# Index keys and head weights in one projection tile, the 64-token output product on both column halves, first modulation chunks copied by ScalarE

## The chip, the cores and the metric

One NeuronCore of one Trainium2 chip runs the whole program; the other cores are idle. The metric is the device time of one execution in microseconds (us), the median over several runs.

## What is computed

The reference is one layer of a hybrid streaming encoder on 512 prompt tokens and 64 sample tokens (the latter with 256 cached positions), model width 1024. In short:

```python
mod = silu(c) @ w_ada + b_ada                      # six vectors of 1024 per stream
h = rmsnorm(x) * (1 + sc1) + sh1
qa, ka, va, qi, ki, wi, qb, kb, vb, qc, kc, vc = split(h @ w_in)
# A: indexer. score[t, s] = sum_h wi[t, h] / sqrt(8) * relu(qi[t, h] . ki[s] / 8), top-k keys, softmax
# B: stick-breaking attention   C: differential attention
x = x + g1 * (concat(oa, ob, oc) @ w_out)
h2 = rmsnorm(x) * (1 + sc2) + sh2
x = x + g2 * (shared expert + top-8 of 64 experts)(h2)
y = rmsnorm(x) * g_final
```

The index keys ki have 64 columns of w_in, the head weights wi 8, and in w_in the 8 stand right behind the 64. The rows of ki, ka, va, kb, vb, kc and vc are outputs too.

## The kernel before

**Layout.** Tokens stand in the free dimension, features in the partitions: h_hi and h_lo (the float32 activations split in two parts) are 128 x 8 x 576. The input projection goes by *tiles* of 128 columns of w_in, named in TILES: first ("ki", 0), then ("wi", 0), four of "qi", and the rest, 30 in all. The tile of ki holds its 64 columns twice, so that both halves of the partitions hold the keys; the tile of wi takes 128 columns of w_in of which only the first 8 are used. Each tile is 48 matmuls of 288 columns (three products of high and low parts, 8 blocks of k, two banks), lines 1457 to 1459.

**Around a tile.** SyncE (SP) loads the weights of 512 KB into a ring of four stages (line 838), ScalarE (ACT) rounds them to w_hi (line 1172), GpSimd (POOL) forms w_lo (line 722; for tile 0 it is VectorE, DVE), TensorE (PE) multiplies, ACT moves both banks to SBUF (line 1214). For a tile whose rows are wanted, PE turns it back to rows with five transposes (lines 1540 and 1544), which wait for both banks to be in SBUF, and ACT takes these out of PSUM (lines 1238 and 1241). make_schedule() writes one order of steps; every engine walks through it and does its own part. The first score step waits for the projection tiles of index queries, and DVE for the rows of wi.

**The first chunks of the modulation.** Before the projection, four chunks n = 0 to 3 give shift and scale of the first norm. For each, PE multiplies silu(c) with 2 MB of w_ada (line 1485; four groups of 32 columns of the array side by side), DVE copies the 128 x 512 result out of PSUM into the single buffer mod_rows (line 2019, shown as run), PE turns it into partitions with matmuls of two columns (line 1496), and DVE adds the bias (line 2032). Then ACT writes h_hi for two blocks (line 1178, four instructions), and DVE computes the same in float32 (hf, line 2038) and the low part h_lo (line 2043). DVE has all of it in one queue: copy(n), modulation(n), the two blocks of n, then copy(n+1). After chunk 1, DVE also forms w_lo of tile 0. The w_ada buffers are three: chunk 3 is loaded into that of chunk 0, after PE has read it (line 821). Of PE, modulation(n), turn(n), modulation(n+1) stand in this order, and projection 0 behind turn(3).

**The output projection.** out_product(t) multiplies o_t with w_out for token tile t (four of 128 tokens, the last, t = 4, of 64), for two halves c of the 1024 columns, into banks (2t + c) mod 4, c outside and k inside (line 1744). DVE multiplies each half by g1 (line 2257, part) and adds it to x (line 2260); ACT then forms the inverse root (line 1350 and on), and DVE the normalized rows h2_rows, which PE turns (line 1755). POOL clears x_got after the last product (wo_full 10, lines 1091 to 1095). Behind this stand the router (line 1769), the choice of experts on DVE (lines 2282 and on), the lists of units, and 72 MoE steps of four units of 32 tokens (lines 1919, 1937, 1955).

Of the kernel before, what the change touches and what calls it, by code (L numbers as in the profile page):

```python
# [14 lines left out]
P = 128  # L15
# [7 lines left out]
HD = 64  # L23
# [106 lines left out]
TILES = ([("ki", 0), ("wi", 0)] + [("qi", i) for i in range(4)]  # L130
# [6 lines left out]
ROWS = ("ki", "wi", "ka", "va", "kb", "vb", "kc", "vc")  # L137
# [12 lines left out]
def make_schedule():  # L150
# [19 lines left out]
    project(TILES[:6])  # L170
    s.append(("cache", "i", 0))
    tiles = list(TILES[6:21])
# [46 lines left out]
    softmax_units([("a", h, t) for t in (1, 2, 3, 4, 0) for h in range(H_A)], TILES[21:27])  # L219
# [4 lines left out]
    project(TILES[27:])  # L224
# [69 lines left out]
def build(nc, io):  # L294

    ctx = ExitStack()
    with ctx:
# [394 lines left out]
        row_sources = [st[1] for st in rows_steps if TILES[st[1]][0][0] in "vw"]  # L692
# [224 lines left out]
        def _(pool):  # L917
# [33 lines left out]
            def store_rows(step):  # L951
                name, j = TILES[step[1]]
                if name == "wi":
                    return
# [32 lines left out]
            def pad(key):  # L987

                g, h, t = key
                if key in (("a", 0, 1), ("c", 0, 0)):  # L990
                    if g == "c":
                        pool.wait_ge(av_done, len(stick_no))
                    pool.wait_ge(proj_taken, 2 * (12 if g == "a" else N_IN))
# [146 lines left out]
        def _(act):  # L1140
# [50 lines left out]
            root()  # L1191
            for q in range(N_FIRST):
                tr.wait_taken(act, ("ada", q))
                modulated(2 * q)
                modulated(2 * q + 1)
                if q == 1:
                    split_high(0)
            split_high(1)

            def evacuate_projection(n):  # L1200
                name, j = TILES[n]
                for b in range(2):
                    act.wait_ge(proj_full, 2 * n + b + 1)
                    if name in ("wi", "va", "vb", "vc"):
# [5 lines left out]
                    else:  # L1210
                        dst = feat(SLOT[name] + j)
                        if b == 0 and name in ("qc", "kc"):
                            qk.wait_full(act, last_score)
                    nc.scalar.activation(dst[:, HALF * b:HALF * b + HALF], bank[b][:, 0:HALF], ACT.Copy,
                                         scale=SCALE_A if name == "qb" else 1.0).then_inc(proj_taken, 1)

            def evacuate_rows(step):
# [3 lines left out]
                if name == "wi":  # L1221
                    w, scale = N_IDX, N_IDX ** -0.5
                    dst = [wi_rows[:, 0:4, :], wi_rows[0:N_SAMPLE, 4, :]]
                elif name[0] == "k":
# [5 lines left out]
                else:  # L1230
# [5 lines left out]
                    dst = [v[:, 0:4, P * j:P * j + P], v[0:N_SAMPLE, 6, P * j:P * j + P]]  # L1236
                tr.wait_full(act, key[0])
# [214 lines left out]
        def _(pe):  # L1452
# [114 lines left out]
            for step in SCHEDULE:  # L1567
# [17 lines left out]
                elif kind == "score":  # L1585
                    t, h = key
                    if t == 1 and h == 0:
                        pe.wait_ge(proj_taken, 2 * 6)
# [7 lines left out]
                elif kind == "qk":  # L1596
                    g, h, t = key
                    if (g, h, t) == ("a", 0, 1):
                        wait_cached("a")
                        pe.wait_ge(proj_taken, 2 * 12)  # L1600
# [136 lines left out]
            def out_product(t):  # L1737
                c0, n = tokens(t)
                for c in range(2):
# [264 lines left out]
        def _(dve):  # L2004
# [10 lines left out]
            def copy_modulation(n):  # L2015
                dve.wait_ge(ada_rows, n + 1 if n < 4 else 4 * (n - 3) + 4)
                if n:
# [541 lines left out]
```

## Time and profile before

| What | Value |
|---|---|
| median of 3 runs | 1239.8 us (1235.46 to 1242.24) |
| the profiled execution | 1229.7 us, its span 1227.7 us |
| PE busy | 1106.3 us, 90% of the span |
| DVE busy | 520.7 us, 42% |
| ACT busy | 371.9 us, 30% |
| POOL busy | 367.3 us, 30% |
| mean granted TensorE clock | 0.975 |

The busy shares are averages over stages; the rows further down give single stretches. Times of rows count from the first instruction of the span. A matmul on float32 operands appears as two instructions in the trace, so that a count of x16 there is eight matmuls of the program.

### The profile page before, as it was taken

To read this page: it belongs to the slowest core of one execution; us is meant where nothing else is said; L and a number is where in the kernel's file an instruction comes from. 1 tells how busy PE (TensorE), PEld (TensorE's weight loads), DVE (VectorE), ACT (ScalarE), POOL (GpSimd) and SP (SyncE) were. 2 spreads that over 40 slices of the span, in tenths; PEclk is the share of its full clock that TensorE was granted. 3 is DMA by queue.
4 is the path that set the end of the run, shared out by engine and by line. 5 is a ranking of instruction groups with operands and counts; after the bars stand their busy time and mean duration, and the time that the engine had idled before them with its cause. 6 is when DMAs were issued, how large, how long until landed. Compare 5 with 4: busy or idle time off the path is not lost.

```text
span 1227.7 us, 24855 instructions
## 1 busy us (share of the span) xinstructions
PE 1106.3 (90%) x9769; PEld 673.1 (55%) x9769; DVE 520.7 (42%) x1293; ACT 371.9 (30%) x908; POOL 367.3 (30%) x464
## 2 busy tenths in 40 slices
PE   3899998899889988899899889999999999999696
PEld 1698896676574555545445444545555555555242
DVE  5517892133426567624552624323233332222155
ACT  3433432233335457601103212222222222222211
POOL 2233333423321043130112423434343434343100
PEclk9899999999999999999989998999999999999898
DMA  9322225633444000030054796969797969676596
GB/s 363 121 86 78 82 80 207 222 109 123 156 172 140 1 1 2 1 112 35 28 221 152 249 376 204 371 251 378 260 377 253 383 241 385 231 297 228 185 422 215
DMA packets 58563, 239.37 MB, mean 195 GB/s; under 512 B 22686, under 2 KB 22766, under 8 KB 46414
## 3 DMA queue, kind: packets, MB, share of 16 engines
q1 hardware_dynamic: 27936, 181.73, 40.2%
q0 software_dynamic: 30512, 56.06, 13.2%
q8 instruction: 78, 1.28, 0.4%
q14 instruction: 37, 0.30, 0.1%
HBM read 292.57 MB, written 47.40 MB: 277 GB/s over the span
## 4 chain that ended last, share of the span: by engine, by line
PE 68%; DMA 16%; DVE 7%; issue 4%; ACT 3%; POOL 2%; SPq 0%; POOLq 0%; DVEq 0%; ACTq 0%
PE bank L1937 14%; PE bank L1955 9%; DMA x_got<-x_dram,idx_tok 8%; PE bank L1744 6%; PE bank L1457 5%; PE bank L1459 5%; PE bank L1458 5%; DMA pairs<-pair_dram 4%; PE bank L1919 4%; PE bank L1563 3%; PE bank L1639 2%; PE bank L1485 1%; PE bank L1683 1%; PE bank L1838 1%; DMA pair_dram<-out_rows,idx_pair 1%
## 5 line engine op out<-in xcount | busy, mean ns | idle before, releaser
L1937 PE MATMUL bank<-slot,xt 128*32 128x256 f32 x4608 | 262.2, 379 | 14.9 <-issue 10.1
L1937 PEld LDWEIGHTS bank<-slot,xt 128*32 128x32 f32 x4608 | 152.5, 110 | 141.8 <-issue 54.3
L1457 PE MATMUL bank<-h_hi,w_hi 128*128 128x288 f32 x480 | 145.3, 303 | 0.0
L1458 PE MATMUL bank<-h_lo,w_hi 128*128 128x288 f32 x480 | 141.7, 295 | 0.0
L1459 PE MATMUL bank<-h_hi,w_lo 128*128 128x288 f32 x480 | 141.6, 295 | 0.0
L1955 PE MATMUL bank<-slot,hid_t 128*32 128x512 f32 x1152 | 139.2, 601 | 0.8 <-ACT hid_t L1424 0.8
L1119 POOL DMA_INDIRECT pair_dram<-out_rows,idx_pair x72 | 73.1, 1016 | 169.0 <-DVE out_rows L2429 156.1
L722 POOL TENSOR_TENSOR w_lo<-w_stage,w_hi 128x1024 fp32r<-128x1024 f32 x29 | 69.6, 2400 | 127.3 <-ACT w_hi L1172 127.3
L2429 DVE COPY out_rows<-bank 128x512 f32<-128x512 f32 x72 | 49.8, 691 | 115.3 <-PE bank L1955 75.0
L1418 ACT ACTIVATE sg<-bank 128x128 f32<-128x128 f32 x72 | 20.0, 277 | 252.0 <-PE bank L1937 251.8
L1457 PEld LDWEIGHTS bank<-h_hi,w_hi 128*128 128x128 f32 x480 | 90.5, 189 | 6.8 <-issue 6.3
L2423 DVE TENSOR_TENSOR hid<-sg,bank 128x128 f32<-128x128 f32 x72 | 20.6, 287 | 169.2 <-ACT sg L1418 160.7
L1458 PEld LDWEIGHTS bank<-h_lo,w_hi 128*128 128x128 f32 x480 | 90.6, 189 | 0.8 <-issue 0.5
L1102 POOL DMA_INDIRECT x_got<-x_dram,idx_tok x72 | 73.3, 1019 | 56.9 <-DVE idx_tok L2400 33.5
L1459 PEld LDWEIGHTS bank<-h_hi,w_lo 128*128 128x128 f32 x480 | 90.4, 188 | 0.0
L1111 POOL DMA_INDIRECT slot<-in_w_moe,idx_w x48 | 49.5, 1032 | 130.0 <-DVE out_rows L2429 76.5
L1919 PE MATMUL bank<-ident,x_got 128*128 128x128 f32 x576 | 76.3, 276 | 11.9 <-DMA x_got<-x_dram,idx_tok 11.8
L1744 PE MATMUL bank<-w_out_sb,o_t 128*128 128x512 f32 (+1 forms) x160 | 71.6, 608 | 2.5 <-DVE o_t L2189 2.5
L1919 PEld LDWEIGHTS bank<-ident,x_got 128*128 128x128 f32 x576 | 65.3, 142 | 15.2 <-DMA x_got<-x_dram,idx_tok 13.9
L1430 ACT COPY out_rows<-bank 128x512 f32<-128x512 f32 x72 | 42.2, 586 | 102.2 <-PE bank L1955 54.4
L2417 DVE COPY xt<-bank 128x512 f32<-128x512 f32 x72 | 49.8, 691 | 53.2 <-PE bank L1919 53.1
L1283 ACT ACTIVATE p_work<-p_work,n_max 128x256 f32<-128x256 f32 (+4 forms) x80 | 44.5, 557 | 62.8 <-DVE n_max L2158 62.6
(366 smaller groups left out, 1537.1 us busy)
## 6 DMA issues: line engine op xcount, KB each, us to landing
slot<-in_w_moe SPq DMA_DIRECT2D x65, 1536.0 KB, 8.7
w_stage<-in_w_ada SPq DMA_DIRECT2D x32, 512.0 KB, 4.4
pairs<-pair_dram SPq DMA_DIRECT2D x16, 1024.0 KB, 9.9
w_stage<-in_w_in SPq DMA_DIRECT2D x30, 512.0 KB, 3.3
resid<-in_w_ada SPq DMA_DIRECT2D x2, 2048.0 KB, 12.9
w_out_sb<-in_w_out SPq DMA_DIRECT2D x1, 4096.0 KB, 14.8
g_bc<-mod_dram SPq DMA_DIRECT2D x6, 512.0 KB, 8.9
o_t<-in_x_t SPq DMA_DIRECT2D x4, 576.0 KB, 5.7
```

The source lines that it names most:

```text
L722: e.tensor_tensor(w_lo[:, n % 2], staged(("w", n)), w_hi[:, n % 2].bitcast(F32), ALU.subtract)\
L1102: g.indirect_dma_start(x_got[:, i % 4, :], None, x_dram, bass.IndirectOffsetOnAxis(ap=idx_tok[:, i:i + 1], axis=0), bounds_check=NT - 1, o ...
L1119: g.indirect_dma_start(pair_dram, bass.IndirectOffsetOnAxis(ap=idx_pair[:, i:i + 1], axis=0), out_rows[:, i % 2, :], None, bounds_check=NT ...
L1457: mm(out, hi_w, hi_x, start=first, stop=False)
L1458: mm(out, hi_w, lo_x, start=False, stop=False)
L1459: return mm(out, lo_w, hi_x, start=False, stop=last)
L1744: ins = mm(bank[i % 4][0:n, :], o_t[:, k, c0:c0 + n], w_out_sb[:, k, 512 * c:512 * c + 512], start=(k == 0), stop=(k == KD - 1))
L1919: ins = nc.tensor.transpose(bank[k // 4][:, P * (k % 4):P * (k % 4) + P], x_got[:, i % 4, P * k:P * k + P], ident[:, :])
L1937: ins = mm(bank[2 + i % 2][r, 0:2 * P], xt[:, i % 2, k, r], slot_of(place_no)[:, 2 * P * k:2 * P * (k + 1)], start=(k == 0), stop=(k == KD ...
L1955: ins = mm(bank[4 + 2 * (i % 2) + c][r, :], hid_t[:, i % 2, r], slot_of(place_no)[:, 2 * D + 512 * c:2 * D + 512 * c + 512], start=True, s ...
L2417: v.tensor_copy(xt[:, i % 2, 4:8, :], bank[1][:, :].rearrange("p (k c) -> p k c", k=4)).then_inc(xt_dve, 1)
L2429: v.tensor_copy(out_rows[:, i % 2, 512:D], bank[5 + 2 * (i % 2)][:, :]).then_inc(out_dve, 1)
```

## The change

Three things change. First, TILES has no ("wi", 0): the tile of ki takes 128 plain columns of w_in from the first of ki on, so that its result holds ki in partitions 0 to 63 and wi in 64 to 71. ACT writes ki from each bank twice (to partitions 0 to 63 and 64 to 127 of its feature slot), and the whole bank into v_t; the turning takes 72 rows of v_t, and ACT takes head weights and keys out of the turned banks separately. Second, the copies of chunks 0 to 3 of the modulation out of PSUM go from DVE to ACT. Third, out_product(4) puts the two halves of the columns into partitions 0 to 63 and 64 to 127 (of two banks), with k outside and c inside. The constants that count tiles follow.

```diff
-TILES = ([("ki", 0), ("wi", 0)] + [("qi", i) for i in range(4)]
+TILES = ([("ki", 0)] + [("qi", i) for i in range(4)]
...
@@ scalar engine, before the projection
+            def copy_modulation(n):
+                act.wait_ge(ada_rows, n + 1)
+                if n:
+                    act.wait_ge(ada_full, n)
+                nc.scalar.copy(mod_rows, tr_bank[tr.bank(("ada", n))][:, :]).then_inc(rows_copied, 1)
+
+            copy_modulation(0)
             for q in range(N_FIRST):
                 tr.wait_taken(act, ("ada", q))
                 modulated(2 * q)
                 modulated(2 * q + 1)
+                if q + 1 < N_FIRST:
+                    copy_modulation(q + 1)
                 if q == 1:
                     split_high(0)
             split_high(1)
@@ evacuate_projection(n)
-                    if name in ("wi", "va", "vb", "vc"):
+                    if name in ("ki", "va", "vb", "vc"):
...
+                    if name == "ki":
+                        for r in (0, HD):
+                            nc.scalar.copy(feat(SLOT["ki"])[r:r + HD, HALF * b:HALF * b + HALF], bank[b][0:HD, 0:HALF])
                     nc.scalar.activation(dst[:, HALF * b:HALF * b + HALF], bank[b][:, 0:HALF], ACT.Copy,
@@ evacuate_rows(step)
+                if name == "ki":
+                    w = HD + N_IDX
+                    tr.wait_full(act, key[0])
+                    both = src[0][:, 0:4 * w].rearrange("p (t c) -> p t c", t=4)
+                    nc.scalar.activation(wi_rows[:, 0:4, :], both[:, :, HD:w], ACT.Copy, scale=N_IDX ** -0.5)
+                    nc.scalar.copy(dst[0], both[:, :, 0:HD]).then_inc(tr_free[tr.bank(key[0])], 1)
...
@@ tensor engine, turn_rows(step)
-                src = feat(SLOT[name] + j) if name[0] == "k" else v_t[:, row_sources.index(n) % 2, :]
-                r = {"wi": N_IDX, "ki": HD}.get(name, P)
+                src = v_t[:, row_sources.index(n) % 2, :] if n in row_sources else feat(SLOT[name] + j)
+                r = HD + N_IDX if name == "ki" else P
@@ out_product(t)
+                if t == 4:
+                    for c in range(2):
+                        pe.wait_ge(part_ready, 5 + c)
+                    for k in range(KD):
+                        for c in range(2):
+                            ins = mm(bank[c][n * c:n * c + n, :], o_t[:, k, c0:c0 + n], w_out_sb[:, k, 512 * c:512 * c + 512],
+                                     start=(k == 0), stop=(k == KD - 1))
+                            if k == KD - 1:
+                                ins.then_inc(wo_full, 1)
+                    return
@@ vector engine
             for q in range(N_FIRST):
-                copy_modulation(q)
                 modulation(q)
...
+                    r = slice(n * c, n * c + n) if t == 4 else slice(0, n)
+                    v.tensor_tensor(part[0:n, c, :], bank[i % 4][r, :], g1_bc[r, stream(t), cols], ALU.mult)\
```

## Rows read from the trace of the kernel before

**Rows 1.** The page: chain of work that ended last, shares by engine.

```profile
PE 68%; DMA 16%; DVE 7%; issue 4%; ACT 3%; POOL 2%; SPq 0%; POOLq 0%; DVEq 0%; ACTq 0%
```

**Rows 2.** Windows: length, busy PE, PEld, DVE, ACT, POOL (xcount), clock, DMA share, GB/s.

```profile
150.00:187.00 37.00, 36.00 (x272) 34.13 (x271) 33.90 (x79) 13.62 (x27) 13.29 (x9) 1.00 0.28 87
523.50:600.80 77.30, 77.30 (x217) 35.51 (x217) 27.63 (x43) 8.26 (x21) 10.15 (x52) 0.97 0.19 65
659.20:1160.00 500.80, 470.21 (x6416) 252.69 (x6416) 162.66 (x389) 120.80 (x288) 188.93 (x185) 0.99 0.78 287
```

**Rows 3.** Chain that ended last, 15 to 61 us: start, length, what.

```profile
23.25 0.70 DVE run L2019
24.00 1.88 PE bank L1496 x8
...
50.81 0.82 ACT resid L1214 x2
```

**Rows 4.** Timeline of PE before the projection: start, length, instruction, [idle before].

```profile
16.80 3.64 PE L1485 MATMUL bank<-resid,silu_c 128*32 128x512 f32 x16 [0.82 <-DMA resid<-in_w_ada]
...
31.42 1.92 PE L1485 MATMUL bank<-ada_third,silu_c 128*32 128x512 f32 x16
...
43.63 1.05 PE L1496 MATMUL bank<-of_stream,run 128*128 128x2 f32 x8 [1.00 <-DVE run L2019]
44.54 0.38 PE L1457 MATMUL bank<-h_hi,w_hi 128*128 128x288 f32 x1
```

**Rows 5.** Window of PE alone: length, busy (xcount), granted clock, DMA share, GB/s.

```profile
40.00:42.00 2.00, 2.00 (x16) 0.50 0.01 4
```

**Rows 6.** Timelines of ACT and DVE, 23 to 40 us.

```profile
26.17 2.18 ACT L1178 ACTIVATE h_hi<-o_t,mod 128x512 fp32r<-128x512 f32 x4 [8.49 <-DVE mod L2032]
...
33.88 1.03 ACT L1172 CAST w_hi<-w_stage 128x1024 fp32r<-128x1024 f32 x1
...
29.02 0.76 DVE L2043 TENSOR_TENSOR h_lo<-hf,h_hi 128x576 fp32r<-128x576 f32 x1
...
35.32 1.22 DVE L722 TENSOR_TENSOR w_lo<-w_stage,w_hi 128x1024 fp32r<-128x1024 f32 x1
```

**Rows 7.** SP timeline, and the same loads' KB and us to landing.

```profile
5.12 0.45 SPq L821 DMA_DIRECT2D ada_third<-in_w_ada  x1
20.48 0.33 SPq L821 DMA_DIRECT2D resid<-in_w_ada  x1
...
ada_third<-in_w_ada SPq DMA_DIRECT2D x1, 2048.0 KB, 23.0
...
resid<-in_w_ada SPq DMA_DIRECT2D x1, 2048.0 KB, 12.6
```

**Rows 8.** Timeline of PE: first matmuls of projection 1 (wi) and of 2.

```profile
52.12 0.40 PE L1457 MATMUL bank<-h_hi,w_hi 128*128 128x288 f32 x1
...
59.62 0.40 PE L1457 MATMUL bank<-h_hi,w_hi 128*128 128x288 f32 x1
```

**Rows 9.** Timeline of ACT: a copy of 128 x 512 out of PSUM.

```profile
630.28 0.59 ACT L1390 COPY unit_value<-bank 128x512 f32<-128x512 f32 x1 [11.01 <-PE bank L1810]
```

**Rows 10.** Groups by form, 586.8 to 601 us: xcount, busy us, mean ns, idle before.

```profile
L1744 PE MATMUL bank<-w_out_sb,o_t 128*64 128x512 f32 x32 | 13.9, 594 | 0.0
L1744 PEld LDWEIGHTS bank<-w_out_sb,o_t 128*64 128x64 f32 x32 | 4.3, 137 | 8.9 <-issue 8.9
```

**Rows 11.** Timeline of PE: one MoE step's down products, four column groups of 32.

```profile
675.96 1.92 PE L1955 MATMUL bank<-slot,hid_t 128*32 128x512 f32 x16
```

**Rows 12.** Timelines of DVE and POOL behind the output projection.

```profile
600.86 0.68 DVE L2257 TENSOR_TENSOR part<-bank,g_bc 64x512 f32<-64x512 f32 x1 [5.46 <-PE bank L1744]
...
604.63 2.51 DVE L2282 TENSOR_SCALAR score<-score 128x64 f32<-128x64 f32 x1 [0.27 <-ACT score L1368]
...
603.58 3.52 POOL L1095 MEMSET x_got<- 128x4096 f32 x1
```

**Rows 13.** The page's groups: turning of the gathered tokens in the MoE stage.

```profile
L1919 PE MATMUL bank<-ident,x_got 128*128 128x128 f32 x576 | 76.3, 276 | 11.9 <-DMA x_got<-x_dram,idx_tok 11.8
```

More of the change, by code:

```diff
@@ L168, in project_with_ada @@
             s.append(("rows", tile[k]))
-    project(TILES[:6])
+    project(TILES[:5])
     s.append(("cache", "i", 0))
-    tiles = list(TILES[6:21])
+    tiles = list(TILES[5:20])
     for t in (1, 2, 3, 4):
@@ L217, in softmax_units @@
             project([k])
-    softmax_units([("a", h, t) for t in (1, 2, 3, 4, 0) for h in range(H_A)], TILES[21:27])
+    softmax_units([("a", h, t) for t in (1, 2, 3, 4, 0) for h in range(H_A)], TILES[20:26])
     s += [("cache", "c", 0), ("cache", "c", 1)]
@@ L223, in make_schedule @@
     s += [("pad",) + units[0], ("pad",) + units[1]]
-    project(TILES[27:])
+    project(TILES[26:])
     for i in range(len(units) + 4):
@@ L690, in softplus @@
             return sp_buf[:, :, :].rearrange("p s c -> p (s c)")[:, c:c + w]
-        row_sources = [st[1] for st in rows_steps if TILES[st[1]][0][0] in "vw"]
+        row_sources = [st[1] for st in rows_steps if TILES[st[1]][0] in ("ki", "va", "vb", "vc")]
         def pad_rows(key, m):
@@ L1236, in evacuate_rows @@
                     dst = [v[:, 0:4, P * j:P * j + P], v[0:N_SAMPLE, 6, P * j:P * j + P]]
+                if name == "ki":
[4 more added lines that the diff above has]
+                    nc.scalar.copy(dst[0], both[:, :, 0:HD]).then_inc(tr_free[tr.bank(key[0])], 1)
+                    tr.wait_full(act, key[1])
+                    nc.scalar.activation(wi_rows[0:N_SAMPLE, 4, :], src[1][0:N_SAMPLE, HD:w], ACT.Copy, scale=N_IDX ** -0.5)
+                    nc.scalar.copy(dst[1], src[1][0:N_SAMPLE, 0:HD]).then_inc(tr_free[tr.bank(key[1])], 1)
+                    return
                 tr.wait_full(act, key[0])
@@ L2108, in _ @@
                         for half in range(2):
-                            tr.wait_taken(dve, ("rows", 1, half))
+                            tr.wait_taken(dve, ("rows", 0, half))
                     qk.wait_taken(dve, step)
@@ L2256, in add_out @@
                     dve.wait_ge(wo_full, i + 1)
-                    v.tensor_tensor(part[0:n, c, :], bank[i % 4][0:n, :], g1_bc[0:n, stream(t), cols], ALU.mult)\
+                    r = slice(n * c, n * c + n) if t == 4 else slice(0, n)
+                    v.tensor_tensor(part[0:n, c, :], bank[i % 4][r, :], g1_bc[r, stream(t), cols], ALU.mult)\
                         .then_inc(part_ready, 1)
@@ L2541 @@
         c = COL[name] + P * j
-        tiles.append(np.concatenate([w_in[:, :, c:c + HD]] * 2, axis=2) if name == "ki" else w_in[:, :, c:c + P])
+        tiles.append(w_in[:, :, c:c + P])
     laid_out["w_in"] = np.stack(tiles).transpose(0, 2, 1, 3).reshape(N_IN, P, D)
```

21 lines of the change are left out of this document (8 added, 13 removed).

## The prediction

> **What bounds the kernel now.** I read the chain that ended last first: 68% of it is TensorE [rows 1]. Then the windows. Between 150 and 187 us, in the stage of scores and top-k, PE is busy 36.0 of 37 us and DVE 33.9; in the output projection PE is busy for all of 77.3 us; in the MoE stage for 470 of 501 us [rows 2]. So what is taken off PE in these stages counts nearly in full. The start is another matter: there the chain goes by turns over DVE's copy out of PSUM (23.25, 0.70 us), PE's turning (24.00, 1.88 us) and DVE's arithmetic [rows 3], and PE stands still between its products [rows 4]. What is saved there counts if projection 0, which starts at 44.54 us [rows 4], starts earlier, since PE is dense from then on. The three parts of the change lie in three places, one behind another, so their effects add.
>
> **Part 1, the first chunks.** Before, copy(n+1) stands on DVE behind all its work for chunk n, and PE cannot turn before it. After, ACT makes the copy; behind it on ACT stand the h_hi of the next chunk, and, behind copy(2), the rounding of tile 0's weights, for which DVE waits. I go through it with the durations of before; ACT's copy of 128 x 512 from PSUM takes 0.59 us [rows 9].
> PE's product of chunk 0 ends at 16.80 + 3.64 = 20.44 [rows 4]; ACT is free, its copy ends at 21.1; PE's turning (1.88) at 23.0. DVE is done with the normalization at 23.25, where its copy began [rows 3], so its bias follows at 23.25, not at 25.9: 2.6 us gained. PE's product of chunk 1 runs from 23.0 to 26.6, the copy to 27.2, the turning (1.05 to 1.88 us by the clock [rows 3, 4]) to 28.3. Chunk 2's weights land at 5.12 + 23.0 = 28.1 [rows 7], in time; its product, 1.92 us at the full clock [rows 4], ends at 30.3. ACT's four h_hi of chunk 1 take 2.18 us [rows 6] and end at 30.8, copy(2) at 31.4, the rounding (1.03) at 32.5. DVE's chunk lasts from 25.88, where the turning ended, to 29.78, that is 3.9 us [rows 3, 6], here from 28.3 to 32.2; then w_lo, 1.22 us [rows 6], to 33.7. PE turns chunk 2 until 32.5. Chunk 3 goes into chunk 0's buffer, whose load is issued at 20.48 in either kernel, since PE's first product does not move, and lands 12.6 us later, at 33.1 [rows 7]; product to 35.0. DVE starts chunk 2 at 33.7, its bias is done at 33.9, h_hi at 36.1, copy(3) at 36.7, turning at 37.8. Projection 0 starts there and not at 44.54: **6.7 us**. The last h_lo, 3.9 us later at 41.7, comes before projection 0 wants the last block of k, 7/8 of its some 6.3 us in, at 43.3.
> The bound on the other side is the clock. From 40 to 42 us the granted clock was 0.50, the 1.2 GHz level, after PE had stood since 33.3 [rows 5, 4]; a product takes 3.64 and a turning 1.88 us at that level. With the low level for chunk 3 alone it ends at 33.1 + 3.64 + 0.6 + 1.9 = 39.3, 5.3 us gained; with the low level from turning 1 on (29.1, 32.8, 33.4, 35.3, 38.9, 39.5, 41.4) 3.1 us. Because the new pauses of PE, 1.0 to 1.3 us, are shorter than those of before, I take 6.5.
> The Trainium skill (TensorE: Matmul & The Clock Gate, the clock gate part) says that the array starts at 1.2 GHz and gets to 2.4 GHz once it was kept busy; the products of 3.64 and of 1.92 us agree, and by that rule the low ends above would need longer pauses than I find.
>
> **Part 2, keys and head weights.** From the first matmul of tile "wi" to that of the next tile are 59.62 - 52.12 = 7.50 us [rows 8]: its 48 matmuls and its turning, both on PE's path. All of it goes, with one rounding on ACT, one w_lo on POOL, one load of 512 KB and two evacuations, which lie beside PE's work: nothing. Added are four ACT copies of 288 columns from PSUM, two for each bank, ahead of the copies into v_t for which the turning waits. PE stands behind them in order, nothing covers this. Two such copies took 0.82 us, the second in part waiting for its bank [rows 3]: 0.41 each, 1.6 in all, is the upper bound; by columns, 0.59 x 288/512 = 0.33 [rows 9], 1.3 in all, the lower. I take 1.4, the middle. The split taking of the turned rows adds nothing on PE's path: the next tile's w_hi begins some 2 us later on ACT, and after 1.03 us there and POOL's w_lo it is wanted only a whole tile later. DVE's wait for the head weights is met sooner, as rows 0 is an earlier step. Part 2: 7.5 - 1.4 = **6.1 us** (5.9 to 6.2).
>
> **Part 3, the output product of 64 tokens.** It takes 13.9 us for 32 instructions, one each 0.434 us, back to back, though it uses 64 of 128 columns [rows 10]. No row shows two groups of 64 columns side by side. The nearest is the MoE down product: 16 instructions of 512 columns in four groups of 32 last 1.92 us [rows 11], 0.12 each against 0.434, so that four run at once. Two groups then give 13.9/2 = 6.95, a gain of 6.9 us; the other end is no overlap at all, gain 0. I take 6.9, since the alternation of groups is that of rows 11. Both halves are now full only at the end, at 593.9, and DVE's first half (two operations of 0.68 us), formerly beside PE's second, comes behind: ACT's inverse root moves by 5.5 us only. But this path is not what ends last: DVE's first operation on the router's scores took 2.51 us, until 607.14, because POOL was clearing x_got until 603.58 + 3.52 = 607.10 [rows 12], and this clearing starts by wo_full 10, so it moves by the full 6.9, to 600.2. The scores, formerly there at 604.6, are there at 599.1, still before it. **6.9 us** reach the choice of experts. The new wait for the banks, for the adds of t = 2, is long met: there is a whole tile of PE work between. That DVE reads partitions 64 to 127 costs nothing: as many columns.
> The Trainium skill (TensorEngine Tiling (Array Packing), Restrictions) speaks against this part: column tiling switches off the fast weight load, and a change of the tiling drains the array. If every one of the 32 loads, 0.137 us each now [rows 10], stood open, 4.4 us would come back and part 3 would give 2.5. In rows 11 the loads of the four groups are hidden.
>
> **Sum.** 6.5 + 6.1 + 6.9 = 19.5 us. In the profiled execution 1229.7 becomes 1210.2; the median of the runs stands 10.1 us above that execution, so I forecast 1239.8 - 19.5 = **1220.3 us**, 1.6% less.
>
> **The rivals.**
> (a) *The halves do not overlap.* Part 3 gives 0: both halves end at 600.8, and ACT's path, 1.4 later, still ends at 606.0, before the clearing. 1239.8 - 12.6 = 1227.2 us. For it: no row with groups of 64. Against: rows 11. 0.08.
> (b) *The weight loads stand open* between the halves: part 3 gives 2.5, 1224.7 us. For it: the loads of 64 columns are twice as wide as those of rows 11. 0.05.
> (c) *The clock stays low in the start*: part 1 gives 3.1, 1223.7 us. 0.10.
> (d) *Hidden anyway*: DVE, 33.9 of 37 us busy in the top-k stage [rows 2], sets its end, and not from the scores' start; then parts 1 and 2 are lost and only 6.9 are left: 1232.9 us. Against: DVE begins with the first scores, which move with the tiles. 0.04.
> (e) *Slower*: the MoE stage. There DMA is busy 78% of the time [rows 2], and PE has waited 11.8 us in all for gathered tokens [rows 13]. The change touches nothing there, but starts it 19.5 us sooner; if the gathers fell otherwise among the weight loads and came later than PE wants them, it would cost. To be slower by 0.5% it must lose 19.5 + 6.2 = 25.7 us, waits three times as long as now, which decides it; at 26 us 1246.3. Against: all issues there hang on PE's and DVE's own progress and move along. 0.03.
>
> **How the numbers follow.** The forecast has 0.70, its own range being 1216 to 1224: part 1 down to 5.3, part 2 5.9 to 6.2, and the spread of the runs shown, 0.3 to 0.4% about their median. The range, 1213 to 1230, takes in (a), (b), (c) and that spread; (d) and (e) are left out. About 0.5% (6.2 us) is what a measurement of this kernel can tell from no change. Faster by more: the forecast, (a), (b), (c), 0.93. Within: (d), 0.04. Slower: (e), 0.03.
>
> **What would show it.** Projection 0 starts near 38 us (41 by (c)); the gap between its last matmul and the first turning is 0.5 + 1.4 us; 29 tiles; the 32 instructions of out_product(4) end in some 7 us (9 to 12 by (b), 13.9 by (a)), and the clearing of x_got ends that much sooner after its start. The distance from the choice of experts to the end stays. A MoE stage of another length, or a projection 0 that starts after 42, would make the prediction wrong.

## The result, and the profile of the changed kernel

The changed kernel takes **1234.1 us** (median of 22 runs, 1218.5 to 1243.1), the kernel before, run beside it, 1240.3 (22 runs, 1232.7 to 1250.8). The ratio is 0.9921 [0.9894, 0.9948]: faster, where 1.6% less was forecast, and outside the range of 1213 to 1230. This ratio leaves out as slow the eight of the 22 changed executions that lie more than 1.5% above the fastest of them, 1218.5, and none of the kernel before, so it flatters the change: the two medians are 6.2 us apart, a ratio of 0.995, and a second series of the changed kernel (again, below) gives 0.9956. So the direction was right, and of the 19.5 us that were forecast some 6 to 7 came. The profiled execution took 1227.08 us, its span 1225.4, against 1229.7 and 1227.7 before.

**First the three places.** The page of the changed kernel, the shares of its chain, and the waits for gathered tokens (before: [rows 1, 13]):

```profile
PE 72%; DMA 16%; DVE 4%; issue 3%; ACT 3%; POOL 2%; SPq 0%; DVEq 0%; POOLq 0%; ACTq 0%
...
L1949 PE MATMUL bank<-ident,x_got 128*128 128x128 f32 x576 | 78.3, 281 | 19.6 <-DMA x_got<-x_dram,idx_tok 19.6
```

PE's timeline, the changed kernel (start us, us, operation, idle before in brackets):

```profile
28.81 3.64 PE L1504 MATMUL bank<-ada_third,silu_c 128*32 128x512 f32 x16 [0.99 <-DMA ada_third<-in_w_ada]
...
34.94 3.64 PE L1504 MATMUL bank<-resid,silu_c 128*32 128x512 f32 x16
...
39.28 1.86 PE L1515 MATMUL bank<-of_stream,run 128*128 128x2 f32 x8 [0.71 <-ACT run L1195]
41.01 0.59 PE L1476 MATMUL bank<-h_hi,w_hi 128*128 128x288 f32 x1
...
51.00 0.47 PE L1559 MATMUL bank<-ident,v_t 72*128 72x72 f32 x4 [2.01 <-ACT v_t L1225]
...
584.15 7.09 PE L1764 MATMUL bank<-w_out_sb,o_t 128*64 128x512 f32 x32
...
596.74 3.45 PE L1799 MATMUL bank<-r_w,h_t 128*128 128x64 f32 x16 [2.69 <-ACT h_t L1377]
```

The timelines of ACT, POOL and DVE, the changed kernel:

```profile
48.63 0.79 ACT L1224 COPY resid<-bank 64x288 f32<-64x288 f32 x2 [4.06 <-PE bank L1478]
49.75 0.78 ACT L1224 COPY resid<-bank 64x288 f32<-64x288 f32 x2
...
593.99 3.52 POOL L1094 MEMSET x_got<- 128x4096 f32 x1
...
596.83 0.72 DVE L2311 TENSOR_SCALAR score<-score 128x64 f32<-128x64 f32 x1 [1.64 <-ACT score L1387]
```

The same turning in the kernel before:

```profile
51.68 0.46 PE L1540 MATMUL bank<-ident,resid 64*128 64x64 f32 x4 [0.50 <-ACT resid L1214]
```

Part 1: projection 0 starts at 41.01 us instead of 44.54 [rows 4], near the 41.4 of case (c), because the later products and the last turning run at 3.64 and 1.86 us, the low level. Part 2: the four copies take 0.79 + 0.78 us, and the gap before the first turning is 2.01 us, 1.5 more than the 0.50 of before. Part 3: 7.09 us for 13.9 [rows 10]. DVE's first operation on the scores takes 0.72 us where it took 2.51 [rows 12].
**Then the stages.** The windows of PE between the same events, before and after (window and its length, busy time, granted clock, DMA share, GB/s): from projection 0 to the first scores, the middle (before only), from the output product to the choice of experts, the lists, the MoE stage, and the sums (before only).

```profile
44.50:86.20 41.70, 40.06 (x304) 1.00 0.24 80
86.20:354.20 268.00, 248.20 (x1669) 0.98 0.37 125
...
523.50:624.30 100.80, 95.28 (x321) 0.96 0.21 68
624.30:659.20 34.90, 34.06 (x127) 0.90 0.61 227
659.20:1165.70 506.50, 470.24 (x6417) 0.99 0.78 286
1165.70:1227.70 62.00, 50.59 (x112) 0.91 0.85 320
```

```profile
41.00:77.90 36.90, 34.26 (x250) 0.96 0.24 75
...
520.60:615.20 94.60, 90.27 (x321) 0.94 0.21 73
615.20:650.20 35.00, 34.12 (x131) 0.90 0.63 228
650.20:1162.50 512.30, 474.23 (x6416) 0.97 0.77 283
```

The scores come 8.3 us earlier (77.9 for 86.2), the choice of experts 9.1, the MoE stage begins 9.0 us earlier, and then it lasts 5.8 us longer (512.3 for 506.5), with the clock at 0.97 for 0.99. "A MoE stage of another length" is among the prediction's own signs of being wrong. In this pair of traces it is the largest single loss, but the profile of the control run below, with nothing changed, has a MoE stage of 510.5 us. One pair of traces does not settle it.

### The profile page after: what moved, and what is told of

It reads as the page before. It is cut to its first block, busy times and chain, and to the rows that moved or that the text cites. A ratio compares the mean times of both kernels' runs of the same rounds, so it can differ in the third digit from the quotient of the medians.

```text
span 1225.4 us, 24745 instructions
## 1 busy us (share of the span) xinstructions
PE 1105.5 (90%) x9716; PEld 672.6 (55%) x9716; DVE 517.3 (42%) x1289; ACT 372.8 (30%) x913; POOL 364.6 (30%) x463
## 4 chain that ended last, share of the span: by engine, by line
PE 72%; DMA 16%; DVE 4%; issue 3%; ACT 3%; POOL 2%; SPq 0%; DVEq 0%; POOLq 0%; ACTq 0%
PE bank L1967 15%; PE bank L1985 9%; DMA x_got<-x_dram,idx_tok 8%; PE bank L1774 5%; PE bank L1949 5%; PE bank L1476 4%; PE bank L1478 4%; PE bank L1477 4%; PE bank L1582 3%; DMA pairs<-pair_dram 2%; PE bank L1658 2%; PE bank L1504 2%; DMA ada_third<-in_w_ada 2%; PE bank L2027 2%; PE bank L1868 2%
## 5 line engine op out<-in xcount | busy, mean ns | idle before, releaser
L1985 PE MATMUL bank<-slot,hid_t 128*32 128x512 f32 x1152 | 142.6, 614 | 0.7 <-ACT hid_t L1443 0.7
L1476 PE MATMUL bank<-h_hi,w_hi 128*128 128x288 f32 x464 | 141.7, 305 | 0.0
L1477 PE MATMUL bank<-h_lo,w_hi 128*128 128x288 f32 x464 | 138.3, 298 | 0.0
L1478 PE MATMUL bank<-h_hi,w_lo 128*128 128x288 f32 x464 | 138.2, 298 | 0.0
L1949 PE MATMUL bank<-ident,x_got 128*128 128x128 f32 x576 | 78.3, 281 | 19.6 <-DMA x_got<-x_dram,idx_tok 19.6
L1985 PEld LDWEIGHTS bank<-slot,hid_t 128*32 128x32 f32 x1152 | 30.7, 111 | 59.2 <-issue 58.1
```

What stands on the lines that cost most here:

```text
L1476: mm(out, hi_w, hi_x, start=first, stop=False)
L1477: mm(out, hi_w, lo_x, start=False, stop=False)
L1478: return mm(out, lo_w, hi_x, start=False, stop=last)
L1949: ins = nc.tensor.transpose(bank[k // 4][:, P * (k % 4):P * (k % 4) + P], x_got[:, i % 4, P * k:P * k + P], ident[:, :])
L1985: ins = mm(bank[4 + 2 * (i % 2) + c][r, :], hid_t[:, i % 2, r], slot_of(place_no)[:, 2 * D + 512 * c:2 * D + 512 * c + 512], start=True, s ...
```

## The experiments

Two figures recur. For every execution the record has the time and the mean granted clock. The **low time** of an execution is 2 x (1 - mean clock) x its time, the us spent at 1.2 GHz. Over the 133 executions of the kernel before (control's and those beside each experiment) the time rises by 0.35 us for each us of low time (correlation 0.81), over 34 of the changed kernel by 0.40 (0.92). I take off 0.40 us for each and call the rest **work**. Such a slope alone does not show that the clock costs the time: a longer wait can add to both. The fillings further down, which take low time away and leave the kernel's own work as it is, are the test of that.

The low time has a gap at the start. In every profile the record of the clock begins at a rise to 2.4 GHz, 16 to 30 us into the span, and the time ahead of it counts as full clock. In before's profile that is at 29.5 us, and there a product takes 3.64 us, the value of the low level, in a window that is given at 1.00:

```profile
24.00:29.00 5.00, 5.00 (x24) 1.00 1.01 429
...
25.80 3.64 PE L1485 MATMUL bank<-feat,silu_c 128*32 128x512 f32 x16
```

Over the ten profiles with DVE's copies the record begins at 23.5 us on average, over the ten with ACT's at 19.2, so some 4 us of a difference in low time between such kernels can be this alone.

The table has means over all executions, with their standard errors. The series ran on five chips, each with the kernel before beside it; its means there lie between 1239.6 and 1242.8 us, and its low time between 87.5 and 97.6. A difference of 1 to 3 us to the pooled mean is therefore less certain than the errors in the table say.

```
kernel              executions   us              low time       work
before and control  133          1240.6 +- 0.5    89.3 +- 1.1   1204.9
changed              34          1233.8 +- 0.9   105.9 +- 2.2   1191.4
only_copies          12          1231.5 +- 1.1    79.0 +- 2.7   1199.8
only_tile            12          1245.2 +- 1.6   106.9 +- 4.4   1202.5
tile_stored          12          1244.8 +- 1.4   110.2 +- 3.1   1200.8
only_halves          12          1237.4 +- 1.8    98.9 +- 4.7   1197.9
tile_held            12          1245.8 +- 1.8    97.8 +- 3.3   1206.7
tile_loaded          12          1241.4 +- 1.3    97.5 +- 3.5   1202.4
before_late          12          1247.7 +- 1.0    90.9 +- 3.0   1211.3
before_plus          12          1240.8 +- 1.9    91.9 +- 3.8   1204.1
halves_filled        12          1234.2 +- 1.2    92.0 +- 2.8   1197.4
warm_start            6          1225.7 +- 2.8    84.6 +- 4.5   1191.9
warm_moe              6          1227.4 +- 2.0    91.7 +- 4.2   1190.7
both_warm             6          1227.9 +- 1.6    87.6 +- 3.7   1192.9
copies_halves         6          1230.5 +- 2.7    92.0 +- 6.2   1193.7
copies_halves_2       6          1233.8 +- 3.5    97.2 +- 7.8   1194.9
copies_halves_warm    6          1230.3 +- 2.2    77.1 +- 4.4   1199.5
all_filled            6          1222.8 +- 2.0    71.8 +- 2.9   1194.1
```

**The parts alone, and the kernel before once more.** Each keeps one part of the diff; for the copies, for example:

```diff
+            def copy_modulation(n):
+                act.wait_ge(ada_rows, n + 1)
+                if n:
+                    act.wait_ge(ada_full, n)
+                nc.scalar.copy(mod_rows, tr_bank[tr.bank(("ada", n))][:, :]).then_inc(rows_copied, 1)
...
             for q in range(N_FIRST):
-                copy_modulation(q)
                 modulation(q)
```

> The kernel before with the first part alone (the first chunks' copies on ACT). Theory A: projection 0 starts 3 to 6.7 us sooner than 44.5, but up to 3 us of it are lost in its own first matmuls at the low clock: the time 0 to 6 us less, ratio 0.995 to 1.000. Rival B: clock low from 24 to 44 us, projection 0 starts at 41, net gain 1 us or none, ratio 0.999 to 1.003.

> The kernel before with the second part alone (keys and head weights in one tile). Theory A: the stretch from projection 0 to the first score product 36 to 36.5 us where it was 41.6 in the profile, with part 2's 6.0 us in it, and the time 6 us less, ratio 0.995. Rival C (a gain ahead of the MoE stage is eaten there by waits for gathered tokens): the same at the scores, but the MoE stage longer and the time less by under 3 us, ratio 0.998 or more.

> The kernel before with the third part alone (the 64-token output product on both halves of the columns). Theory A: 7.1 us for the 32 instructions, the clearing of x_got 6.8 us sooner after the start of the output projection, and the time 6.8 us less, ratio 0.9945. Rival C: the same up to the choice of experts, then a longer MoE stage, ratio 0.998 or more.

> The kernel before, unchanged, as its own control. The 35 executions of it that ran beside the last four kernels had a mean granted clock of 0.965, that is 88 us at the low level (twice 1 - clock, times the time), and 1240.7 us on average; the profile that the prediction went by had 0.975, 61 us and 1229.7. Theory D (that profile was a lucky execution, and MoE waits for gathered tokens of 17 to 23 us are the rule of both kernels): ratio 0.998 to 1.002, and in this profile the MoE stage is 510 to 519 us (506.5 in the first) with waits of 15 us or more. Rival B (the changed kernels bring the waits): the MoE stage again near 506 us with 12 us of waits.

> The changed kernel once more, to see what of its profile is the same in another execution. Theory A (the three gains are real, and the granted clock falls otherwise in each execution): the stretch from the start of projection 0 to the first score product again 36 to 37 us, 41.6 before; the 32 instructions of the 64-token product again 7.1 us, 13.9 before; but the start of projection 0 between 38 and 41.5 us and the low-clock stretches elsewhere than in the first profile, and the time between 1218 and 1240 us. Rival B (the change itself brings the low clock and the longer waits for gathered tokens): the clock is 0.50 again from about 24 to 44 us and from 509 to 526 us, the waits for gathered tokens are again near 20 us (12 before), and the time 1230 to 1240 us.

Ratios to before: copies 0.9941 [0.9911, 0.9971], tile 1.0043 [1.0006, 1.0081], halves 0.9969 [0.9932, 1.0005], control 0.9998 [0.9966, 1.0030], the whole change again 0.9956 [0.9922, 0.9990]. From the means: copies -9.1 us, tile +4.4 (with tile_stored, which differs only in memory), halves -3.2; their sum, -7.9, agrees with the -6.8 of the whole. So the effects do add, about, and the terms of tile and halves are wrong. In work they are -5.1, -3.3 and -7.0, near the forecast 6.5, 6.1 and 6.9 for the first and the last; the rest goes with low time: -10, +19 and +10 us of it. The whole change has 16.5 us more low time than before, at 0.40 us each 6.6 us given back, of 13.5 of work.

The windows of PE of the control, at the start and for the MoE stage:

```profile
24.00:44.00 20.00, 16.31 (x72) 0.50 0.66 269
...
660.10:1170.60 510.50, 471.29 (x6416) 0.98 0.78 284
```

And of only_tile, from projection 0 to the scores, the middle, the MoE stage and the sums:

```profile
44.50:81.60 37.10, 34.45 (x251) 0.95 0.24 75
81.60:350.40 268.80, 247.27 (x1669) 0.98 0.37 125
...
655.90:1174.90 519.00, 477.28 (x6416) 0.97 0.76 279
1174.90:1238.20 63.30, 50.92 (x112) 0.93 0.83 313
```

In the tile alone the stage up to the scores is 4.6 us shorter, as part 2 says, the middle 0.8 longer, the MoE stage 12.5 longer than in before's profile and 8.5 longer than in the control's, the sums 1.3 longer. But the length of the MoE stage says little about the tile: over all twenty profiles it goes from 506 to 521 us, and the ten without the merged tile average 513.4 us, the ten with it 515.3; before_late below, without it, has 520.6.

**Where the tile's loss comes from.** First where w_in lies in memory: the merged tile drops one of 30 tiles, and everything stored behind could move. tile_stored keeps 30 in memory and skips one.

```diff
-                src = io["w_ada"][n // 4][:, D * (n % 4):D * (n % 4) + D] if kind == "ada" else io["w_in"][n]
+                src = io["w_ada"][n // 4][:, D * (n % 4):D * (n % 4) + D] if kind == "ada" else io["w_in"][n + (n > 0)]
...
+        if name == "ki":
+            tiles.append(w_in[:, :, COL["wi"]:COL["wi"] + P])
```

> The kernel with the merged tile alone, but w_in stored with its 30 tiles as before, the second never read, so that all tensors lie in DRAM where they lay. The merged tile alone had 107 us at the low clock on average against 88 before, and a ratio of 1.004 where its own gain was to give 0.995. Theory E (the place of the expert weights in DRAM is what makes transfers and so PE's pauses longer): low clock back to about 88 us, ratio 0.995. Theory A (the earlier start only shifts the stages against the clock's rise and fall, the place is of no matter): low clock again 100 to 110 us, ratio 1.000 to 1.006.

1.0030 [0.9994, 1.0065], mean 1244.8: the same loss. The place in memory is out.

Then whether PE time ahead of the MoE stage counts at all. tile_held is only_tile, and before_late the kernel before, each with one more tile's 48 matmuls on PE, into a bank that nobody reads. They take 6.4 us at 2.4 GHz; the 7.50 us of [rows 8] hold the turning too. The edit of tile_held (before_late has the same ahead of projection 2):

```diff
+                    if step[1] == 1:
+                        pe.wait_ge(w_lo_ready, 2)
+                        for b in range(2):
+                            for k in range(KD):
+                                three(bank[4][:, 0:HALF], w_hi[:, 1, k, :], w_lo[:, 1, k, :],
+                                      h_hi[:, k, halves(b)], h_lo[:, k, halves(b)], k == 0, k == KD - 1)
```

> The kernel with the merged tile alone, but with the removed tile's 48 matmuls made all the same (same operands' shapes, into a bank nobody reads) behind projection 0, so that PE's time to the scores is the old one. The merged tile alone took 1245.0 us on average over 24 executions against 1240.7 of the kernel before, with 109 us at the low clock against 88. Theory G (it is the earlier position of all later stages, that is another phase of the same pauses, which brings the low clock): low clock back to 85 to 92 us, time 1241 to 1243. Theory H (something else in the merged tile, its copies or the pause behind projection 0): low clock stays 100 to 110 us, and the time is the 6.4 us of these matmuls above it, 1250 to 1252.

> The kernel before with 48 more matmuls of a projection tile (dense, into a bank nobody reads) ahead of projection 2, which takes 6.4 us of PE. The kernel before is at 1241.1 us on average. Theory A (PE's time ahead of the MoE stage counts in full): 1246.5 to 1248.5, low clock 86 to 94 us. Theory K (the MoE stage's length depends on the execution and on how the stages meet the clock's changes so strongly that some 6 us ahead of it do not show): 1240 to 1244.

before_late: 1.0058 [1.0030, 1.0086], +7.1 +- 1.1 us, and its low time is that of before. PE time there counts in full, 7.1 for 6.4. tile_held: 1.0023 [0.9987, 1.0059], mean 1245.8. Giving the merged tile these 6.4 us of PE back costs 0.8 +- 2.1 us, with 10.8 us less low time: the saving is there, and low time comes with it. Neither expectation fits whole: the low time came down as theory G says, the time did not. Against the pooled mean tile_held is 5 us above before, with 8 us more low time; against the 17 executions of before on its own chip it is 3.0 +- 2.2 us above, with the same low time (0.3 +- 4.0 us more). So it is not shown that anything else in the merged tile costs.

Then the number of transfers. before_plus adds one load of 512 KB to the kernel before (ACT waits for it much later, ahead of the first kb tile), tile_loaded to only_tile, which thus has as many as before:

```diff
+                if i == 4:
+                    sp.wait_ge(ada_rows, 2)
+                    sp.dma_start(feat2[:, :, :].rearrange("p k n -> p (k n)")[:, 8 * NT - D:8 * NT], io["w_in"][0])\
+                        .then_inc(extra_in, 16)
```

> The kernel before with one more transfer of 512 KB on SP's queue, early, into columns that are free then, and nothing else. Theory L (the number of transfers on that queue ahead of the MoE stage changes how its transfers run): the mean moves by 3 us or more either way, or the low clock by 10 us or more. Otherwise: 1239.5 to 1242.5, low clock 86 to 94 us.

> The merged tile alone, with the transfer it saves still made, at the same place in SP's queue as in before_plus. The merged tile alone: 1245.0 us on average, low clock 109 us. Theory L: back to the 1235 to 1237 us that its 6 us of PE time should give, low clock about 90. Otherwise: 1243 to 1247, low clock 100 to 110.

0.9994 [0.9957, 1.0030] and 1.0025 [0.9992, 1.0059]. On before it does nothing; on only_tile the mean is 3.6 us less than with both forms of the tile, two standard errors, and each against before on its own chip it is 2.4 us less, about one: not enough to name a cause.

One candidate shows in the traces, and no run tests it: the longer pause behind projection 0. With the clock at 1.00 throughout, the stretch from projection 0 to the scores takes 41.6 us without the merged tile and 35.5 with it, 6.1 less. Before is in [rows 4] and in the windows above; tile_stored has

```profile
43.70:79.20 35.50, 32.93 (x249) 1.00 0.24 79
```

But of the seven profiles with the merged tile whose projection 0 runs at full speed (tile_held aside, which has other work there), four have 3.4 us of low clock just behind this pause, and their stretch takes 37.1 us, like only_tile's:

```profile
53.15 0.34 PE L1550 MATMUL bank<-ident,v_t 72*128 72x72 f32 x2 [2.01 <-ACT v_t L1216]
...
53.50:56.50 3.00, 3.00 (x15) 0.50 0.13 37
```

None of the five such profiles without the merged tile has it; there the pause is 0.50 us. That is about 0.9 us on average; what the tile loses beyond it stays open.

**Fillings on the changed kernel.** Matmuls on constants, written to a bank that is overwritten before anybody reads it, keep PE busy where it waits anyway. warm_start has them in the pauses between the first chunks, warm_moe at one wait for gathered tokens:

```diff
+            def busy(out, n):
+                for _ in range(n):
+                    mm(out, neg_ones[:, :], ident[:, :], start=True, stop=True)
+            busy(bank[4][:, 0:P], 4)
             for n in range(N_FIRST):
                 modulation(n)
+                busy(bank[4][:, 0:P], 3)
                 turn_modulation(n)
+                busy(bank[4][:, 0:P], 3 if n < N_FIRST - 1 else 0)
...
             def turn_x(i):
+                if i == 11:
+                    pe.wait_ge(xt_act, i)
+                    pe.wait_ge(xt_dve, i)
+                    for _ in range(28):
+                        mm(bank[0][:, 0:P], ident[:, :], ident[:, :], start=True, stop=True)
```

> The changed kernel with matmuls whose result nobody reads (128 x 128 constants, 4 ahead of the first modulation product, 3 behind each product and each turning but the last), so that PE does not pause there. If it is the low clock that takes back part 1's gain: the clock is 1.00 from chunk 1 on, a modulation product takes 1.9 us, projection 0 starts by 38.5 us with matmuls at full speed, and the time is 4 to 6 us less than that of the changed kernel, ratio to before 0.991. If the clock does not follow this filling: start of projection 0 at 41 to 43, time as the changed kernel or 1 to 2 us more.

> The changed kernel with 28 such matmuls (6 us at the full clock) ahead of the turning of MoE step 11, where PE waits 8 us for gathered tokens and the clock is low for 10 us behind it. If that pause is what brings the low clock: no low stretch behind step 11, on average 10 us less at the low clock than the changed kernel's 106, and 2.5 to 5 us less time. If the low clock there has another cause: low stretch as before, time unchanged within 1 us.

> The changed kernel with both fillings, at the start and ahead of MoE step 11. Alone they had 1225.7 and 1227.4 us on average against 1233.8 of the changed kernel. If both fillings act by the low clock they remove: 1219 to 1222 us on average, low clock near 70 us (85 and 92 alone), ratio to before 0.983.

Ratios to before: 0.9892 [0.9838, 0.9946], 0.9884 [0.9828, 0.9940], 0.9885 [0.9840, 0.9930]. Against the changed kernel that is -8.1 +- 2.9, -6.4 +- 2.2 and -5.9 +- 1.8 us, with 21, 14 and 18 us less low time, and the work is the same as the changed kernel's within 1.5: what the fillings gain goes with the low time that they remove, at about the slope of above. The two together show no more than each alone, where 1219 to 1222 us were expected. In warm_start's own profile 6.8 us of low clock stay (from 26.7 us), and projection 0 starts at 39.2, not by 38.5; in both_warm's it starts at 38.0. In the changed kernel's windows the wait at step 11 of the MoE stage is followed by low clock:

```profile
720.00:725.00 5.00, 1.00 (x17) 0.83 1.02 424
725.00:730.00 5.00, 0.91 (x4) 0.50 0.98 392
730.00:735.00 5.00, 5.00 (x41) 0.65 0.30 103
```

and its timeline has the wait itself, 8.09 us for the gather:

```profile
729.09 1.97 PE L1949 MATMUL bank<-ident,x_got 128*128 128x128 f32 x8 [8.09 <-DMA x_got<-x_dram,idx_tok]
```

The same rows with the filling (warm_moe) show a high clock where the filling runs, and low later, in the rest of the wait:

```profile
725.00:730.00 5.00, 5.00 (x63) 1.00 0.99 413
735.00:740.00 5.00, 3.73 (x20) 0.66 0.45 158
```

The kernel before has this wait too (control: 8.08 us at 739.55). It was not made by the change. All profiles without this filling have 6.8 to 10.2 us of low clock in and behind it, but for before_late, which waits 3.95 us there and has 3.4; the four with the filling have 3.4 or none.

**Parts 1 and 3 without part 2.** If part 2 loses some 4 us, leaving it out should win.

> The first and the third part without the merged tile. If the parts' measured effects add (copies -9.2 us, halves -3.3, tile +4.3 against the mean of the kernel before, 1240.7): 1228 us on average, 5.6 us less than the whole change (1233.8), low clock near 90 us. If each part's raw effect is only the luck of its stages' positions and the work saved is what counts: 1236 to 1240 us, slower than the whole change by the 4.3 to 6 us that the tile saves.

> The first and third part without the merged tile once more, for more executions: 1230.5 us on average over the first six. If leaving the tile out is worth what the single parts said: 1228 to 1231, below the whole change's 1233.8. If not: 1233 to 1238.

> The first and the third part with both fillings and without the merged tile. If the merged tile costs time in itself: 5 us less than with it (both_warm). If the tile only shifted pauses: 4 to 6 us more than both_warm.

The first gave 0.9898 [0.9840, 0.9956], but its second series, for which the record has no ratio, a mean of 1233.8; the 12 together 1232.1, which can't be told from the changed kernel's 1233.8. With the fillings, 0.9886 [0.9837, 0.9934], 2.4 +- 2.8 us more than both_warm with part 2: it has 77.1 us of low time for 87.6, while its work is 6.6 higher, about part 2's forecast. (Without the fillings the work differs by 2.9 only, 1194.3 for 1191.4, so work does not add up exactly either.) So the tile loses when it is alone, and I could not show that it loses beside the other parts.

**Part 3's own pause.** halves_filled is only_halves with

```diff
             turn_h2(3)
+            pe.wait_ge(part_ready, 8)
+            for _ in range(11):
+                mm(bank[3][:, 0:P], ident[:, :], ident[:, :], start=True, stop=True)
             route(3)
```

> The third part alone with 11 matmuls on constants (2.3 us at the full clock, result read by nobody) in the pause of PE behind the turning of h2 tile 3, where it waits 2.7 us for ACT. In both kernels with this part and the low clock profiled as 17.1 us there, the lists' stage took 40.0 us, not 35.0. If this pause brings that low clock: no low stretch at 594 to 600 us, the lists' stage 35.0 us, low clock 88 to 92 us on average (98.9 without the filling), time 1233.5 to 1235 (1237.4 without). If not: 40.0 us again, time 1237 to 1239.

The same place in PE's timeline of the kernel before:

```profile
604.53 2.00 PE L1769 MATMUL bank<-r_w,h_t 128*128 128x64 f32 x16 [0.90 <-ACT h_t L1358]
```

PE's timeline, and windows of PE that begin there and at the lists, of only_halves:

```profile
599.27 3.67 PE L1780 MATMUL bank<-r_w,h_t 128*128 128x64 f32 x16 [2.69 <-ACT h_t L1358]
...
595.00:615.00 20.00, 17.07 (x92) 0.83 0.37 92
600.00:605.00 5.00, 5.00 (x17) 0.50 0.00 0
617.70:657.70 40.00, 39.12 (x131) 0.79 0.55 199
```

And of halves_filled, a window and the timeline:

```profile
595.00:615.00 20.00, 18.33 (x130) 1.00 0.39 118
...
599.44 2.62 PE L1847 MATMUL bank<-ident 128*128 128x128 f32 x22
602.29 2.00 PE L1780 MATMUL bank<-r_w,h_t 128*128 128x64 f32 x16 [0.23 <-ACT h_t L1358]
```

Before, PE waited 0.90 us for h_t. With 7 us less of product in front of this place it waits 2.69, since ACT's evacuation, inverse root and scaling are as long as they were. Behind it the clock is at 0.50 from 600 to 605; with the pause filled it stays at 1.00, and the router's product takes 2.00 us for 3.67. From the output product to the MoE stage it was 135.7 us before, 129.6 in the best profiles with the halves, and 134.2 in only_halves, where the stage of the lists took 40.0 us at a clock of 0.79 (for 34.9 at 0.90); six of the nine profiles with the halves unfilled have this 40.0, and the other three have 35.0. Over the nine the whole stretch averages 132.6 us, 3.1 less than before, about what part 3 brought in time (3.2). With the filling it is 128.5, and 128.7 in all_filled. Over the executions the filling takes 3.2 us off (1234.2 for 1237.4, with a standard error of 2.2 on the difference; 0.9952 [0.9922, 0.9983] to before), about as much as part 3 fell short by (3.7), though by the times alone it is not certain.

**All fillings on the changed kernel** (both_warm and this one):

> The changed kernel with all three fillings (start, behind the turning of h2 tile 3, ahead of MoE step 11). If each takes its low clock away: 1221 to 1225 us on average, low clock under 80 us, ratio to before 0.985. If the clock only falls elsewhere instead: 1226 to 1229, as with one or two fillings (1225.7, 1227.4, 1227.9), low clock 85 to 92 us.

0.9851 [0.9800, 0.9901], mean 1222.8, 17.8 us below before, low time 71.8. It is 11.0 +- 2.2 us below the changed kernel with 34 us less low time, 0.32 us for each. It beats both kernels.

## Why the prediction was wrong, and where it was right

**The reading of the bound** stands at an unchanged clock: in before_late, whose low time is that of before, 6.4 us more of PE ahead of the MoE stage cost 7.1 +- 1.1 us.

**Part 1** holds in its steps and by more than its size: 6.5 forecast, 3.5 in the profile, 5.3 in the mean (six profiles with the copies and no filling at the start, ten without the copies), 9.1 us in the time of only_copies (of which 5.1 is work). Its steps come out where the clock is high: in both_warm, at 1.00 from 24 to 44 us, projection 0 starts at 38.0 us, where the prediction had 37.8. Case (c), the low clock at the start, came about in this profile, and the argument against it failed: "Because the new pauses of PE, 1.0 to 1.3 us, are shorter than those of before, I take 6.5." They were shorter still, 0.3 to 1.0 us in this profile, and the clock was low all the same. The control, with the pauses of before, was at the low level from 24 to 44 us as well; so this varies from one execution to the next. The profile of before was itself at the high level only from 29.5 to 36.4 us, with the product of 1.92 us in it. A term left out: the first 12 matmuls of projection 0 ran at 0.24 us instead of 0.133 in the changed kernel, 1.3 us (24 of them in only_copies, 2.6 us).

**Part 2**: 6.1 forecast, and 6.1 us is what the stretch up to the scores loses at the full clock (41.6 to 35.5 us), the gap being 1.5 us against 1.4. And yet +4.4 us in the time. The term that failed is what the change does to the clock, for which the prediction has nothing: there are 106.9 and 110.2 us of low time for 89.3, and of the work 3.3 us are saved, not 6.1. The runs did not find the path: it is not the place in memory, and the number of loads is not shown to be it. In the MoE stage the profiles of only_tile and tile_stored have 36.1 and 30.6 us of low time, before and control 13.1 and 20.7; but before_late, without the tile, has 30.8, so this does not place it.

**Part 3**: the halves overlap entirely (7.09 for 6.95), cases (a) and (b) are out. The rule of the Trainium skill (TensorEngine Tiling (Array Packing), Restrictions) that column tiling switches off the fast weight load shows no cost here: the 32 loads take 137 ns each in either kernel, and the product's time is halved. DVE's multiplication out of partitions 64 to 127 takes 0.69 us, as the prediction has it (0.68). The steps on ACT and on POOL's clearing hold, 593.99 + 3.52 us. What failed is "6.9 us reach the choice of experts": 6.2 us do in the profile (94.6 for 100.8), but behind them low clock takes back, and of the whole term 3.2 us are left. ACT's path "moves by 5.5 us only" is in the prediction's own text; that PE would then stand for 1.8 us more than before, and what follows on the clock, it did not ask.

**The MoE stage**: what case (e) describes is seen in a small size: 5.8 us longer in the profile, waits of 19.6 us for 11.8 [rows 13]. But the control waits 18.2 with nothing changed, and the other profiles without a filling at step 11 wait 16.8 to 23.1, so I can't lay those waits to the change; the profile of before was the odd one.

**The sum.** The step that failed is "So what is taken off PE in these stages counts nearly in full", with the sum of 19.5 us that rests on it: it has no term for what the change does to the clock, outside the start. The change brought 16.5 us more low time (105.9 for 89.3), which at 0.40 us for each is 6.6 us given back (5 us, if 4 us of it are the gap at the start). Of the 12.7 us that are missing (6.8 for 19.5) that is about half. The rest, 6 us or more, is missing in work, 13.5 for 19.5; alone, part 2 falls short in it most (3.3 for 6.1) and part 1 a little (5.1 for 6.5), and their cause is open. The profile that the prediction took its clock from could not show this: it had 61 us of recorded low time, below all 133 others (64 to 126), though with one of the longest gaps at the start, and its 1229.7 us stood 11 us under their mean. The prediction saw 10 us of that and carried them over as a constant, which left its base right. That the direction came out right owes something to the copies, which brought 9.1 us for 6.5 and had 10 us less low time, as nothing in the prediction foresaw.

## What to carry to other kernels

Before a saving is costed on PE, ask what pause it opens: work taken from in front of a wait lengthens the wait, and a pause can cost more behind it than in itself (here 1.8 us more of pause, and 5 us behind it in six of nine profiles). Compare mean clocks over many executions before a few us are explained from two traces, check the clock column at the start against the durations of like instructions, and cost a stage at both levels. Where a pause can't be closed, matmuls on constants inside it kept the clock up: with three such fillings 11 us here, more than the 6.8 that the change itself brought.

## What the hardware showed that I had not expected

- From 24 to 44 us PE of the changed kernel is busy for 16.9 of 20 us, with no pause over 1.0 us, and at 0.50 all the time:

```profile
24.00:44.00 20.00, 16.90 (x76) 0.50 0.66 268
```

  With fillings (both_warm) the same stretch is at 1.00:

```profile
24.00:44.00 20.00, 17.49 (x139) 1.00 0.65 269
```

- The same kernel spends 64 to 126 us of its 1240 at the low level, and two thirds of the variance of its time go with this (0.81 squared).
- Two groups of 64 columns with 512-column f32 matmuls run side by side at full rate: 0.222 us each for 0.434.
- ACT's copies of 64 x 288 out of PSUM back to back take 0.39 us each.
